# Scatter one-hots of an expert layer: gated ones on GpSimd per token, plain ones on VectorE for eight tokens, and 70 early expert rows in place of 42

## What is computed

```python
eidx = ...                      # 8 heads x 16 experts for each token: i * 128 + j
g = jax.nn.softmax(top_s, axis=-1)
u = u_tab[eidx]
act = jax.nn.gelu(jnp.einsum('chkd,cd->chk', u, xb), approximate=False)
w = (g * act).astype(xb.dtype)
return jnp.einsum('chk,chkd->cd', w, v_tab[eidx])
```

## Time and profile before

| | us |
|---|---|
| median of 3 runs | 2046.31 |
| lowest and highest run | 2044.93, 2048.76 |
| the profiled execution | 2046.0 |
| its span in the profile | 2044.2 |
| PE, DVE, ACT, POOL busy | 1985.2, 1490.9, 979.3, 1072.0 |

### The profile page before, as it was taken

How to read it: one execution, slowest core, us unless ns; L and a number is a source line. 1 busy time by engine, 2 the same in 40 slices (tenths; PEclk the granted TensorE clock), 3 DMA queues, 4 the chain that set the end, 5 groups by cost and what they waited for, 6 DMA issues and landing times.

```text
span 2044.2 us, 31709 instructions
## 1 busy us (share of the span) xinstructions
PE 1985.2 (97%) x11783; PEld 1771.3 (87%) x11783; DVE 1490.9 (73%) x2883; ACT 979.3 (48%) x1805; POOL 1072.0 (52%) x646
## 2 busy tenths in 40 slices
PE   9999999998999999999999999999999999999998
PEld 8746889998999999999999999999877787877787
DVE  6237538989998388889889999987686635067763
ACT  4337434366788643333333333333556652255643
POOL 3213456865446577776767777674335444411242
PEclk9999999999999999999999999999999999999999
DMA  5330225767679899999999999996322222210021
GB/s 206 81 101 12 74 92 169 260 214 234 236 238 331 316 357 410 399 404 373 365 379 390 412 380 407 365 403 241 117 71 93 83 93 103 94 40 32 21 83 62
DMA packets 155144, 446.78 MB, mean 219 GB/s; under 512 B 14960, under 2 KB 60912, under 8 KB 152816
## 3 DMA queue, kind: packets, MB, share of 16 engines
q1 hardware_dynamic: 108912, 276.96, 38.4%
q0 software_dynamic: 46080, 167.79, 21.2%
HBM read 405.39 MB, written 39.31 MB: 218 GB/s over the span
## 4 chain that ended last, share of the span: by engine, by line
PE 69%; DVE 14%; DMA 6%; issue 5%; POOL 3%; ACT 2%; SPq 0%; DVEq 0%; ACTq 0%
PE bank L528 12%; PE bank L530 12%; PE bank L529 12%; PE bank L934 4%; PE bank L935 4%; PE bank L936 4%; PE bank L915 3%; DMA fetched<-in_u_rows,diag 3%; DVE fetched L2384 2%; POOL wl L2725 2%; DVE wide L2404 2%; PE bank L1156 2%; PE bank L703 1%; POOL fetched L2848 1%; DMA fetched<-in_v_rows,diag 1%
## 5 line engine op out<-in xcount | busy, mean ns | idle before, releaser
L2725 POOL TENSOR_TENSOR wl<-wraw,wh 128x1024 fp32r<-128x1024 f32 x272 | 667.5, 2458 | 660.7 <-ACT wh L1347 658.6
L1347 ACT CAST wh<-wraw 128x1024 fp32r<-128x1024 f32 x360 | 373.3, 1046 | 141.4 <-PE bank L530 109.8
L528 PE MATMUL bank<-WTH,wh 128*128 128x352 f32 x1024 | 336.9, 329 | 22.6 <-issue 22.0
L529 PE MATMUL bank<-WTL,wh 128*128 128x352 f32 x1024 | 334.4, 327 | 0.0
L530 PE MATMUL bank<-WTH,wl 128*128 128x352 f32 x1024 | 334.3, 326 | 0.0
L528 PE MATMUL bank<-AXH,wh 128*128 128x352 f32 (+1 forms) x832 | 299.3, 360 | 5.9 <-issue 4.9
L530 PE MATMUL bank<-AXH,wl 128*128 128x352 f32 (+1 forms) x832 | 294.9, 354 | 0.0
L529 PE MATMUL bank<-AXL,wh 128*128 128x352 f32 (+1 forms) x832 | 294.8, 354 | 0.0
L528 PEld LDWEIGHTS bank<-WTH,wh 128*128 128x128 f32 x1024 | 194.8, 190 | 29.5 <-issue 28.8
L934 PE MATMUL bank<-AXH,wh 128*128 128x352 f32 x576 | 191.8, 333 | 6.6 <-issue 6.6
L529 PEld LDWEIGHTS bank<-WTL,wh 128*128 128x128 f32 x1024 | 194.8, 190 | 0.0
(11 more groups left out here) (557 smaller groups left out, 4109.3 us busy)
## 6 DMA issues: line engine op xcount, KB each, us to landing
wraw<-in_wstream SPq DMA_DIRECT2D x360, 512.0 KB
g_scratch<-gs SPq DMA_DIRECT2D x11, 2048.0 KB, 9.8
gr<-g_scratch SPq DMA_DIRECT2D x15, 1408.0 KB
a_scratch<-tmp SPq DMA_DIRECT2D x72, 176.0 KB
tmp<-a_scratch SPq DMA_DIRECT2D x44, 176.0 KB
sq<-a_scratch SPq DMA_DIRECT2D x28, 176.0 KB
shifted<-hc_scratch SPq DMA_DIRECT2D x12, 270.0 KB, 4.8
h<-in_hT SPq DMA_DIRECT2D x8, 264.0 KB, 5.8
```

The lines of the kernel that those rows point to most:

```text
L528: pe.matmul(o, w1, x1, start=n == 0, stop=False)
L529: pe.matmul(o, w1, x2, start=False, stop=False)
L1347: act.copy(wh[n % NSPLIT][:, :], wraw[n % NRAW][:, :]).then_inc(*w_hi.tell(n))
L2725: return pool.tensor_tensor(lo, src, hi.bitcast(F32), ALU.subtract)
```

## The change

POOL now makes the gated i one-hot itself: one operation per token, 128x128, that compares a row of 0..127 with the token's i and multiplies by its gate, into one of four buffers `hots_gated` (`below_XL` and `sq`). It waits for the scatter of quad q-4. DVE makes only the j one-hots, for two quads at once (128x1024, two buffers), and waits for the scatter of quad q-3. ACT's multiplications go. The early picks go from 42 to 70: 10 before loop 1, then 14, 14 and 32, and 255 entries in place of 283 are left for the expert stage.

```diff
-EARLY_PICKS, LEAD, NEARLY, NFETCH = 42, 4, 3, 6
+EARLY_PICKS, LEAD, NEARLY, NFETCH = 70, 4, 3, 6
...
-                while picks < (10, 18, 26)[tt - 1] + (8, 8, 16)[tt - 1] * now // whole:
+                while picks < (10, 24, 38)[tt - 1] + (14, 14, 32)[tt - 1] * now // whole:
...
-            def gate(q):
-                act.wait_ge(*hot.at(q))
-                for t in range(4 * q, 4 * q + 4):
-                    act.mul(hots[q % 4][0][:, t % 4, :], hots[q % 4][0][:, t % 4, :],
-                            ijgT[:, 2, t:t + 1]).then_inc(*hot_gate.tell(t))
...
+            for q in hots_at(t0)[::2]:
...
+                    dve.wait_ge(*scat_mm.at(q - 3))
...
+                dve.tensor_tensor(hots[q // 2 % 2][:, :, :], iota_psum.unsqueeze(1).to_broadcast([128, 8, 128]),
+                                  ijgT[:, 1, 4 * q:4 * q + 8].unsqueeze(2).to_broadcast([128, 8, 128]),
+                                  ALU.is_equal).then_inc(*hot.tell(q, q + 1))
...
+            for q in hots_at(t0):
+                if q == EXTRA // 4 or q % 32 == 0:
+                    pool.wait_ge(*ijg_made.at(1 + q // 32))
+                if q > 3 + EXTRA // 4:
+                    pool.wait_ge(*scat_mm.at(q - 4))
+                for t in range(4 * q, 4 * q + 4):
+                    pool.tensor_scalar(hots_gated[q % 4][:, t % 4, :], iota, ijgT[:, 0, t:t + 1], ijgT[:, 2, t:t + 1],
+                                       ALU.is_equal, ALU.mult).then_inc(*hot_gate.tell(t))
```

More of the change, by code:

```diff
@@ L281, in build_program @@
     gs = [sb(B, f"gs{i}", [128, 128, 32]) for i in range(2)]
[L282 to L286, removed]
+    hots = [sb(B, f"hots{i}", [128, 8, 128]) for i in range(2)]
+    hots_gated = [below_AXL[:, 0:4, 0:128], below_AXL[:, 4:8, 0:128]]
+    hots_gated += [x[:, 0:512].rearrange("p (i c) -> p i c", i=4) for x in sq]
     gates = ijg[:, 2, :].rearrange("p (h k) -> p h k", h=8)
@@ L912, in scatter @@
                 bank_of["scat", q] = bank = banks[2 + q % 2]
+                pe.wait_ge(*hot.at(q))
                 for i in range(4):
                     pe.wait_ge(*hot_gate.at(4 * q + i))
-                    mm = pe.matmul(bank[:, i * 128:i * 128 + 128], hots[q % 4][1][:, i, :], hots[q % 4][0][:, i, :],
+                    mm = pe.matmul(bank[:, i * 128:i * 128 + 128], hots[q // 2 % 2][:, 4 * (q % 2) + i, :],
+                                   hots_gated[q % 4][:, i, :],
                                    start=True, stop=True, skip_group_check=True)
@@ L1612, in scatter @@
                          bank_of["scat", q][:, :].rearrange("p (t i) -> p i t", t=4)).then_inc(*scat_out.tell(q))
-            for q in hots_at(t0):
-                if q >= now + 2:
-                    gate(q)
         spilled = [0]
@@ L2326, in scatter @@
                 if q > 3 + EXTRA // 4:
[L2327 to L2342, removed]
+                    dve.wait_ge(*scat_mm.at(q - 3))
+                if q == 34:
+                    dve.wait_ge(*ld_e.at("all"))
+                    dve.scalar_tensor_tensor(eidx2, shared[:, 0:EXTRA], 128.0, shared[:, EXTRA:2 * EXTRA], ALU.mult,
+                                             ALU.add).then_inc(*routed.tell((1, "experts")))
+                    dve.tensor_reduce(token_of, ident.rearrange("p (t a) -> p t a", a=SHARED), AX.X,
+                                      ALU.add).then_inc(*routed.tell((1, "token")))
+                dve.tensor_tensor(hots[q // 2 % 2][:, :, :], iota_psum.unsqueeze(1).to_broadcast([128, 8, 128]),
+                                  ijgT[:, 1, 4 * q:4 * q + 8].unsqueeze(2).to_broadcast([128, 8, 128]),
+                                  ALU.is_equal).then_inc(*hot.tell(q, q + 1))
         spilled = [0]
@@ L2819, in scatter @@
         def scatter(t0):
-            pass
+            for q in hots_at(t0):
[6 more added lines that the diff above has]
+                                       ALU.is_equal, ALU.mult).then_inc(*hot_gate.tell(t))
         spilled = [0]
```

3 lines of the change are left out of this document (removed).

## The result

The changed kernel takes 2259.43 us (median of 4 runs, 2252.96 to 2260.79) against 2046.65 us (2044.93 to 2048.76) of the kernel before: ratio 1.1028, 95% interval 1.1011 to 1.1045. The forecast was 2052 us with a range of 2026 to 2074; it missed by 207 us.

A forecast was written before the change was run, and what follows sets the result against it. PE, busy 97% of the span, was taken as the bound, with loop 3 becoming bound by POOL. Loops 1, 2 and 3 at +2, +2 and +19, expert stage -17: +6 on 2046.0 gives 2052 us, range 2026 to 2074.

The forecast's parts named there:

- a row of another operation on the same engine: POOL's one-hot in the loops, scaled from rows of a fill, a square and a difference: 0.28 us, range 0.22 to 0.39.
- the blocking: DVE picks and POOL contending for SBUF in the loops: 4 us in loop 3, 8 us each in loops 1 and 2.
- room on average: POOL in loop 2: 86 of 93 us, fits on average; with waits for picks 95, so +2 us.
- one-input operations on GpSimd at roughly line rate: Rival for POOL's one-hots in the loops: cheap, 0.22 us or less, whole kernel 2030 us; chance 0.34.

## What to carry over

Before work is moved to another engine, measure that very operation there, with its comparison, its second step and its width; a row of another operation on the same engine is no upper bound, and what is multiplied by 352 is worth a run of its own. Where two engines share a way into SBUF, charge the blocking to both, above all to the one that becomes the bound: count the operations of the other (beside 58 picks of 1.2 us it was held up for 59 us here, some 50 of them by the picks; beside 32 picks for 39). And room on average is not room: POOL was half idle, and 88 operations of 0.78 us still cost 0.4%.

## What the runs showed of the chip

- On GpSimd, compare and multiply on 128x128 float32 takes 0.78 us, 64 columns 0.57, 8 columns 0.38: 0.36 us and 3.3 ns per column. A comparison without the multiplication takes 0.59, addition and multiplication 0.44. The Trainium skill (GPSIMD Engine Reference, "Engine selection") has, in its row on add, mul and max, one-input operations on GpSimd at roughly line rate; for the comparison with a multiplication the measurement, 3.3 ns per column, decides against that, and for an addition no run shows the rate per column. DVE made eight such one-hots, without the gate, in 1.23 us.
- Constants instead of two pointers to per-partition values save 0.07 us of the 0.78: eight in a row take 5.68 us against 6.22.
- With two SBUF operands a pick on DVE takes 1.75 us on average beside a busy GpSimd, up to 5.3; with one in PSUM 1.22, never over 1.23. GpSimd's own 0.78 us operations become 0.95 and 0.81 us in the same two kernels.
